# Two-layer diffusion backbone on one core: joins, squares and four adaLN slabs at the end of layer 0's experts

## The reference, cut to what matters

```python
for l in range(DEPTH):
    sh1, sc1, g1, sh2, sc2, g2 = split(silu(c) @ w_ada[l] + b_ada[l], 6)     # and the same of c_ctx
    h_lat = rms_norm(x, norm1_g[l]) * (1 + sc1) + sh1                        # h_ctx from ctx likewise
    h_ctx = rms_norm(ctx, norm1_g[l]) * (1 + csc1) + csh1
    y_lat, y_ctx = parallel_mixer(h_lat, h_ctx, w_in[l], ...)                # starts with h @ w_in[l]
    x = x + g1 * y_lat
    h2 = rms_norm(x, norm2_g[l]) * (1 + sc2) + sh2
    x = x + g2 * grouped_moe(h2, ...)      # 16 experts, the best 2 of a token's group; layer 0: ctx too
return rms_norm(x, final_g)
```

## Time and profile before

| | us |
|---|---|
| median of 3 runs (lowest, highest) | 1657.58 (1657.3, 1658.45) |
| the profiled execution | 1655.31 |
| its span, first to last instruction | 1653.4 |
| PE busy | 1495.7 (90%) |
| DVE / ACT / POOL busy | 817.5 / 616.7 / 233.7 |
| mean clock granted to PE | 0.959 of full |

### The profile page before, as it was taken

One profiled execution on the slowest core, in us unless ns is written; L12 is line 12 of the kernel. 1 busy time (PEld: TensorE's weight loads), 2 busy tenths in 40 slices (PEclk: granted clock), 3 DMA queues, 4 the chain that ended last, 5 costly groups with the idle time before them and its releaser, 6 DMA issues.

```text
span 1653.4 us, 16629 instructions
## 1 busy us (share of the span) xinstructions
PE 1495.7 (90%) x6502; PEld 959.8 (58%) x6502; DVE 817.5 (49%) x1111; ACT 616.7 (37%) x823; POOL 233.7 (14%) x204
## 2 busy tenths in 40 slices
PE   4999999998999967999999669999989987998884
PEld 1444665455888836888878434476548864433331
DVE  3145980676734457888887344482573123111103
ACT  3223441266333256778777242341151022111102
POOL 0004970400000002112110100281500000000000
PEclk8999999999999978999999879999999998999997
DMA  9511015395121546999999841114361456999991
GB/s 358 191 52 51 1 52 153 120 386 208 51 102 51 204 153 232 392 400 398 400 401 399 293 180 58 47 56 124 81 254 52 153 203 222 394 395 393 395 392 72
DMA packets 167142, 352.09 MB, mean 213 GB/s; under 512 B 21776, under 2 KB 22928, under 8 KB 167056
## 3 DMA queue, kind: packets, MB, share of 16 engines
q1 hardware_dynamic: 145472, 331.52, 54.1%
q0 software_dynamic: 3456, 12.58, 2.1%
q10 hardware_dynamic: 18128, 6.82, 2.0%
HBM read 339.38 MB, written 11.53 MB: 212 GB/s over the span
## 4 chain that ended last, share of the span: by engine, by line
PE 84%; DVE 6%; issue 3%; DMA 3%; ACT 2%; POOL 1%; SPq 0%; DVEq 0%; ACTq 0%; POOLq 0%
PE bank L543 15%; PE bank L554 7%; PE bank L1139 6%; PE bank L596 5%; PE bank L1161 4%; PE bank L916 3%; PE bank L922 3%; PE bank L913 3%; PE bank L620 3%; PE bank L514 2%; PE bank L733 2%; PE bank L736 2%; PE bank L729 2%; PE bank L1172 2%; PE bank L835 2%
## 5 line engine op out<-in xcount | busy, mean ns | idle before, releaser
L543 PE MATMUL bank<-hT,ring 128*128 128x512 f32 (+1 forms) x768 | 256.4, 492 | 10.2 <-ACT hT L1474 7.0
L2536 DVE TENSOR_TENSOR slab_lo<-slab,high 128x4096 fp32r<-128x4096 f32 x48 | 211.8, 4418 | 7.0 <-ACT high L1748 6.5
L543 PEld LDWEIGHTS bank<-hT,ring 128*128 128x128 f32 x768 | 146.8, 192 | 116.4 <-issue 98.9
L1748 ACT ACTIVATE high<-slab 128x4096 fp32r<-128x4096 f32 x48 | 174.3, 3635 | 26.0 <-PE bank L922 13.1
L1139 PE MATMUL bank<-narrow_slab,picked 128*64 128x512 f32 x256 | 114.4, 600 | 11.8 <-issue 11.6
L1140 PE MATMUL bank<-narrow_slab,picked 128*64 128x512 f32 x256 | 114.6, 601 | 0.0
L2011 POOL DMA_INDIRECT feed_rows<-token_table,slot_token x16 | 42.6, 2665 | 502.5 <-DVE slot_token L2476 307.8
L554 PE MATMUL bank<-ring,hT 128*128 128x512 f32 x256 | 110.5, 592 | 0.0
L596 PE MATMUL bank<-hT,ring 128*128 128x512 f32 (+1 forms) x256 | 104.7, 548 | 0.0
L554 PEld LDWEIGHTS bank<-ring,hT 128*128 128x128 f32 x256 | 48.6, 190 | 60.4 <-issue 60.3
L1139 PEld LDWEIGHTS bank<-narrow_slab,picked 128*64 128x64 f32 x256 | 34.7, 138 | 82.7 <-issue 82.2
(11 more groups left out here) (302 smaller groups left out, 2609.1 us busy)
## 6 DMA issues: line engine op xcount, KB each, us to landing
ring<-in_w_ada SPq DMA_DIRECT2D x24, 2048.0 KB, 13.0
ring<-in_w_in SPq DMA_DIRECT2D x24, 2048.0 KB, 9.0
slab<-in_w_gate SPq DMA_DIRECT2D x16, 2048.0 KB, 15.9
slab<-in_w_up SPq DMA_DIRECT2D x16, 2048.0 KB, 15.0
slab<-in_w_down SPq DMA_DIRECT2D x16, 2048.0 KB, 14.7
narrow_slab<-in_w_gate SPq DMA_DIRECT2D x16, 2048.0 KB, 18.0
narrow_slab<-in_w_up SPq DMA_DIRECT2D x16, 2048.0 KB, 22.0
narrow_slab<-in_w_down SPq DMA_DIRECT2D x16, 2048.0 KB, 19.3
```

What stands on the lines that cost most here:

```text
L543: mm = T.matmul(o[:, lo:TOK], w[:, k, c * P:(c + 1) * P], hT[:, k, lo:TOK], start=(k == 0), stop=(k == KT - 1))
L1748: S.activation(high[kind][:], w[:], ACT.Copy)\
L2536: V.tensor_tensor(low[:], w[:], high[kind][:].bitcast(f32), ALU.subtract)\
```

## The change

- The four adaLN slabs 16 to 19 leave the list `loads`. The slots that came free for them at the end of the experts now take `("in", 1, 3)` to `("in", 1, 6)`. The adaLN slabs get buffers of their own, `ada_slab`, over tiles that are dead by then; SP issues them after the gathers have landed, the fourth after the last join too, since it lies over `tok_rows[1]`. They signal in pairs: `ada_there0` for 16 and 17, `ada_there1` for 18 and 19.
- On PE the rows of 16 and 17 come after the transposes of `join_tokens` and ahead of `mean_square`; the rows of 18 and 19 and the turns of 16 and 17 after `mean_square` and ahead of the first projection; the turns of 18 and 19 after its first column block. ACT copies 16 and 17 after the root and 18 and 19 after `hT`; DVE adds all four to `mod` after the norm.
- DVE does all four joins ahead of both additions.
- The squares of this one norm are made by segments (16 pieces of 128x256, as soon as each piece of `xT` is there), and GpSimd sums them (14 additions) in place of DVE (7).
- Three semaphores of the kernel's start become one, `filled`, counted to three.

The diff, cut to its core:

```diff
@@ -229,6 +229,9 @@
...
     high = [fixed(f"high{i}", [P, SLOT], f32r, offset=(A0 + 44 * KB, A0 + 60 * KB, hT_at)[i]) for i in range(3)]
+    ada_slab = [fixed(f"ada_slab{i}", [P, SLOT], offset=A0 + (44, 60, 0, 76)[i] * KB) for i in range(4)]
+    square_late = fixed("square_late", [P, 2, TOK], offset=A0 + 32 * KB)
+    sum_late = fixed("sum_late", [P, TOK], offset=A0 + 36 * KB)
     hrow = fixed("hrow", [P, 4, D], offset=A0)
...
@@ -280,6 +283,15 @@
...
+        late_ada = range(16, 20)
...
+        def squares_before(count):
...
+            return KT * count + (KT if count > 2 else 0)
...
+        def sums_before(count):
+            return (KT - 1) * count + (KT - 1 if count > 2 else 0)
...
         def slot_of(key):
...
@@ -287,9 +299,6 @@
...
         for l in range(DEPTH):
-            if l == 1:
-                loads += ada_loads[16:20]
-                lane += range(SLOTS)
             loads += [("in", l, s) for s in (3, 4, 5, 6, 0, 1, 2, 7)]
...
@@ -506,21 +515,26 @@
...
                 key = ada_loads[n]
-                pe.wait_ge(*full(key))
-                w = slot(key).rearrange("p (k n) -> p k n", k=KT)
+                if n in late_ada:
+                    pe.wait_ge(sem[f"ada_there{(n - 16) // 2}"], 32)
+                    w = ada_slab[n - 16][:].rearrange("p (k n) -> p k n", k=KT)
+                else:
+                    pe.wait_ge(*full(key))
+                    w = slot(key).rearrange("p (k n) -> p k n", k=KT)
                 o = open_bank(key, "ada_row")
...
                 mm.then_inc(sem["psum_ready"], 1)
-                slot_spent[slot_of(key)] = (sem["psum_ready"], jobs[0])
+                if n not in late_ada:
+                    slot_spent[slot_of(key)] = (sem["psum_ready"], jobs[0])
...
                 if n == 0:
-                    pe.wait_ge(sem["pick2_ready"], 1)
+                    pe.wait_ge(sem["filled"], 3)
                 for j in range(4):
...
@@ -529,8 +543,8 @@
...
                 o = open_bank(key, "norm_std")
-                pe.wait_ge(sem["square_added"], (KT - 1) * (count + 1))
-                T.matmul(o[:, lo:TOK], ones, square_sum[:, lo:TOK], start=True, stop=True).then_inc(sem["psum_ready"], 1)
+                pe.wait_ge(sem["square_added"], sums_before(count + 1))
+                T.matmul(o[:, lo:TOK], ones, (sum_late if count == 2 else square_sum)[:, lo:TOK], start=True, stop=True).then_inc(sem["psum_ready"], 1)
...
@@ -569,10 +583,18 @@
...
                     ada_turn(3)
+                else:
+                    ada_rows(18)
+                    ada_turn(16)
+                    ada_rows(19)
+                    ada_turn(17)
                 for s, who in ((3, "q_ready"), (4, "k_sig"), (5, "k_sig")):
...
                         project(l, s, c, who, lo if s == 3 else 0)
+                        if l and s == 3 and c == 0:
+                            ada_turn(18)
+                            ada_turn(19)
                 pe.wait_ge(*full(("in", l, 6)))
...
@@ -1248,14 +1270,6 @@
...
                 if l == 0:
...
-                    pe.wait_ge(sem["y_kept"], 2 * N_EXPERTS)
-                    pe.wait_ge(*total(1, None, "x_added", phases[1][1] - 1, 4))
-                    for n in range(16, 20):
-                        ada_rows(n)
-                        if n > 16:
-                            ada_turn(n - 1)
-                    ada_turn(19)
                     join_tokens()
...
@@ -1263,7 +1277,12 @@
...
                         continue
-                    reader["experts", l, b] = ("tok_added", 16)
+                    reader["experts", l, b] = ("tok_added", 8 if b < 4 else 16)
+                if l == 0:
...
+                    turns[0] = 0
+                    ada_rows(16)
+                    ada_rows(17)
             if stop > 30:
...
@@ -1299,6 +1318,11 @@
...
                         sp.wait_ge(sem[f"tok_there{t}"], 32)
+                    for i in range(4):
+                        if i == 3:
+                            sp.wait_ge(sem["tok_joined"], 4)
+                        sp.dma_start(ada_slab[i][:].rearrange("p (k n) -> p k n", k=KT), source(ada_loads[16 + i])[0])\
+                            .then_inc(sem[f"ada_there{i // 2}"], 16)
                 while n < base:
...
@@ -1352,7 +1376,9 @@
...
-                    first_after = {i: slot_of(ada_loads[16 + i]) for i in range(SLOTS)}
+                    first_after = {i: min(m for m in range(slot_of(("in", 1, 3)), len(loads)) if lane[m] == i)
+                                   for i in range(SLOTS)}
+                    assert sorted(first_after.values()) == [slot_of(("in", 1, 3)) + i for i in range(SLOTS)]
                     for e in range(-1, N_EXPERTS):
...
@@ -1460,6 +1486,9 @@
...
                         .then_inc(sem["square_ready"], 1)
+                finish_norm(key, count, lo)
...
+            def finish_norm(key, count, lo):
                 act.wait_ge(*is_ready(key))
...
@@ -1491,12 +1520,28 @@
...
                 segs = segs_of[l]
-                norm(("ms", l, 0), 2 * l, 0, lambda k: (sem["tok_added"], KT + k + 1))
...
                 if l == 0:
+                    norm(("ms", 0, 0), 0, 0, None)
                     for n in range(4):
                         ada_keep(n)
+                else:
...
+                    act.wait_ge(sem["filled"], 2)
+                    S.activation(unused_std[:], epsv[:], ACT.Sqrt)
+                    for sg in range(2):
+                        for k in range(KT):
+                            act.wait_ge(sem["tok_added"], KT * sg + k + 1)
+                            if k >= 2:
+                                act.wait_ge(sem["square_added"], sums_before(2) + (KT - 1) * sg + max(1, k - 2))
+                            a = slice(sg * SEG, (sg + 1) * SEG)
+                            S.activation(square_late[:, k % 2, a], xT[:, k, a], ACT.Square).then_inc(sem["square_ready"], 1)
+                    finish_norm(("ms", 1, 0), 2, 0)
+                    ada_keep(16)
+                    ada_keep(17)
                 modulate(2 * l, 0, gain1[:, l], mod[:, l, 0:KT, :])
+                if l:
+                    ada_keep(18)
+                    ada_keep(19)
                 for c in range(4):
...
@@ -1938,8 +1983,6 @@
...
                 if l == 0:
-                    for n in range(16, 20):
-                        ada_keep(n)
                     join_tokens()
...
@@ -2024,6 +2067,15 @@
...
+                for sg in range(2):
+                    a = slice(sg * SEG, (sg + 1) * SEG)
+                    for k in range(1, KT):
+                        pool.wait_ge(sem["square_ready"], squares_before(2) + KT * sg + k + 1)
+                        if k > 1:
+                            pool.wait_ge(sem["square_added"], sums_before(2) + (KT - 1) * sg + k - 1)
+                        G.tensor_tensor(sum_late[:, a], square_late[:, 0, a] if k == 1 else sum_late[:, a],
+                                        square_late[:, k % 2, a], ALU.add).then_inc(sem["square_added"], 1)
...
@@ -2056,7 +2108,7 @@
...
             by_row = ident.rearrange("p (j c) -> p c j", c=32)
-            V.tensor_reduce(pick2[:], by_row[:, 0:2, :], AX.X, ALU.add).then_inc(sem["pick2_ready"], 1)
+            V.tensor_reduce(pick2[:], by_row[:, 0:2, :], AX.X, ALU.add).then_inc(sem["filled"], 1)
...
@@ -2119,8 +2171,6 @@
...
                 if l == 1:
-                    for k in range(KT):
-                        add_square(2, k, 0)
                     invert(2, 0)
...
@@ -2129,6 +2179,9 @@
...
                 link(V.memset(pb[:, :, 0:1], 0.0))
+                if l:
+                    for n in late_ada:
+                        ada_mod(n)
                 for way, (k_to, p_to) in enumerate(((kf, pf), (kb, pb))):
...
@@ -2580,11 +2633,9 @@
...
-                    join(0)
-                    join(1)
-                    join(2)
+                    for t in range(4):
+                        join(t)
                     add(0)
-                    join(3)
                     add(1)
...
@@ -2761,8 +2812,6 @@
...
                 if l == 0:
-                    for n in range(16, 20):
-                        ada_mod(n)
                     join_tokens()
```

More of the change, by code:

```diff
@@ L254, in build @@
     expert_table = nc.dram_tensor("expert_table", (N_EXPERTS * P, D), f32, kind="Internal").ap()
-    names = """const_loaded vec_loaded x_loaded tables_loaded bias_loaded out_stored psum_ready side_ready cond_zeroed cond_ready
-        pick2_ready ada_row ada_mod
-        epsv_ready lower_ready square_ready square_added norm_std normed_ready h_ready q_ready
+    names = """const_loaded vec_loaded x_loaded tables_loaded bias_loaded out_stored psum_ready side_ready filled cond_ready
+        ada_row ada_mod
+        lower_ready square_ready square_added norm_std normed_ready h_ready q_ready
         sig_ready k_sig log_in log_out v_ready naqk_ready rope_done sums_ready decay_in decay_out fac_ready
@@ L269, in build @@
```

(16 more changed lines are left out.)

## The result

| | before | with the change |
|---|---|---|
| median (lowest, highest), 9 runs each | 1657.48 (1653.22, 1658.49) | 1662.93 (1657.2, 1669.03) |
| the profiled execution, its span | 1655.31, 1653.4 | 1666.41, 1664.6 |
| mean clock granted to PE, profiled execution | 0.959 | 0.953 |

The ratio is 1.0038 with a 95% interval of 1.0021 to 1.0055: slower, by 5.5 us in the medians and 6.3 us by the ratio (interval 3.5 to 9.1), where 4.2 was forecast. Beside the last experiments the same kernel gave 1.0020 (1.0005 to 1.0034; median 1662.49 of 12 runs against 1658.98 of 30). The two intervals overlap between 1.0021 and 1.0034, or 3.5 to 5.6 us, and the forecast lies in that.

What follows compares the result with a forecast made beforehand. TensorE bounds the kernel (84% of the span); locally, PE waiting for late adaLN slabs moves the second block of layer 1's first projection from 975.1 to 979.3. That +4.2 on the 1657.6 median gives 1661.8 us, range 1659.4 to 1663.8.

Steps and rivals of the forecast that it cites:

- the fourth landing: Last of the four late adaLN transfers, expected at 966.3 us; rows 18 and 19 wait for it ahead of the projection.
- the half clock: After PE's idling before rows 18, PE was expected at half clock for 4.1 us from their start.
- xT complete, against before: End of the last additions into xT, expected at 950.9 instead of 953.6 us through joins first: 2.7 us earlier.
- rows 16 and 17: PE's adaLN rows ahead of the mean-square matmul, starting at the second landing near 955.5 and taking 6.1 us.
- mean-square matmul ends, against before: Matmul of the norm's summed squares, held behind PE's queue, expected to end at 962.7 instead of 961.8: 0.9 us later.
- rows 18, turn 16, rows 19, turn 17: PE's adaLN work ahead of layer 1's first projection, starting at 966.4 and expected to end at 973.9 us.
- marker: Start of the second column block (c = 1) of layer 1's first projection, expected at 979.3 instead of 975.1: +4.2 us.
- GpSimd's sums: The norm's 14 additions of squares, taken at 0.75 us each, expected to end at 956.0 us, 3.6 earlier than before.
- the second (slabs in time, pauses hide the rows): Slabs arrive in time at layer 1's start and the sums set the end: -1.8 us, 1655.8; chance 0.04.
- The first rival: PE's clock stays up through the pause at 963 to 966, or something later recovers part: +2.2 to +3.2; chance 0.14.
- The third (all four transfers land together): The four adaLN transfers share engines and end together at 966.3, delaying rows 16 and 17: +13.5 us, 1671; chance 0.03.
- The fourth rival (sums as the bound): GpSimd's additions, at 1.59 us each, end at 967.8 and set the projection's start: +9.9 us, 1667.5; chance 0.04.

Runs made afterwards that it cites:

- e1: The changed kernel with the four adaLN slabs loaded, read and turned where they were before the change; ratio 0.9992 against before, median 1657.19 us.
- e2: The kernel before with only the late adaLN slabs and their moved PE rows; joins, squares and sums as before; 1.0027 against before, median 1662.25 us.
- e4: The changed kernel with rows 16 to 19 reading w_in slabs already in the ring, without the adaLN transfers; 2682.74 us, unusable because routing changed.
- e7: The changed kernel's order on PE, ACT and DVE, but the four adaLN slabs stay in the ring as before; 0.9998 against before, median 1658.22 us.
- e3: The changed kernel with the rows of slabs 16 and 17 moved behind the mean-square matmul on PE; 1.0009 against before, median 1660.69 us.
- e5: The kernel before with one edit, all four joins ahead of both additions; 0.9978 against before, median 1656.09 us.
- e6: e1 with the squares in eight buffers and the sums shared by GpSimd and DVE; 0.9969 against before, median 1655.22 us.

## Why the prediction was right

The forecast was +4.2 us, 1661.8, by PE's rows waiting for the slabs' landings, with the second landing ahead of the mean square and the fourth ahead of the projection. e1, e2, e4 and e7 show this cause from both sides: take the slab part out, or its waits alone, and the loss is gone; keep it alone, and the loss is there in full. What e3 adds is that the loss has two parts, the wait for the fourth landing and the half clock behind the pause; the forecast had both. How near the number came is partly luck, since the two comparisons of the change with before, 5.5 and 3.5 us in the medians, themselves lie 2 us apart. Step by step, counted from the expert's end, so that an earlier shift doesn't enter:

| step | forecast | profile after |
|---|---|---|
| xT complete, against before | -2.7 | -2.9 |
| last sum, against before | -3.6 | -1.2 |
| landings 2 and 4, after the first issue | 13.6, 24.4 | 13.7, 25.4 |
| rows 16 and 17 | 6.1 | 6.4 |
| mean-square matmul ends, against before | +0.9 | +1.4 |
| rows 18, turn 16, rows 19, turn 17 | 7.5 | 9.0 |
| block 0, then turns 18 and 19 | 3.5, 1.9 | 3.6, 1.7 |
| marker | +4.2 | +6.6 (again: +5.0) |

Three terms were mis-sized. *The fourth landing* came 25.4 us after the first issue and not 24.4, in both profiles of the change; this is 1.0 of the 2.4 us by which the marker in the first profile lies behind the forecast, and its cause is open (e3 has 24.4). *GpSimd's sums* I took at 0.75 each; they came every 0.87 from start to start, each with a busy time of 0.72, and DVE's additions had no part in it, since the second seven, with DVE idle, took as long as the first. So the rule on the shared port in the Trainium skill, "SBUF — State Buffer", didn't come into play: the additions read one of their inputs from PSUM. (The prediction's working by that rule has a slip: 0.75 and 0.40 make 1.15 a sum and not 1.0, so 961.6 for the last sum, just ahead of the 961.7 at which rows 16 and 17 were to end.) Behind the first sum of each half there is another wait of 0.6 for ACT's square. It cost nothing here because the sums weren't what PE waited for, and 1.6 us in e1 against e5. *The half clock* behind the pause I ended 4.1 us after the start of rows 18; it ended 7.6 after it in one profile and 3.7 in the other. I had it at half from their start. In the first profile PE began rows 18 at full clock, fell to half 0.8 us later and stayed there until 976.6, though it was busy all the time; in the second the fall came 0.3 us after the start. My value lay near the second profile, my upper bound, +5.4, was 1.2 short of the first.

Of the rivals, the second (slabs in time, pauses hide the rows) said what e4 and e7 then measured: with the data there, the pieces fit, and the sums and hT set the end. Its price of -1.8 us was too good, +0.3 and +1.0 in the profiles, since it counted on the sums at 956.0. The first rival's bound, 10.9 us from the fourth landing to the marker at full clock, is e3's 11.0. The third (all four transfers land together) didn't occur: the landings came in order, 5.4 to 6.3 us apart. The Trainium skill, "DMA: Bandwidth & Descriptors", in "Queues, rings and completion order", leaves the order of completion open; the landings of this case came in order. The fourth rival (sums as the bound) didn't occur either.

The profiled executions differ by 11.2 us, of which the stage explains 6.6. Another 1.5 lie ahead of it, and 3.1 behind it. The first part is no sign of the change: the end of the expert's work lies between 919.9 and 923.4 us in the ten profiles, 922.4 and 923.4 in the change's two, but 920.3 in e2, which has the same slab part. Most of the last part can be placed. First and last start of the two groups around layer 1's second norm and router, before:

```profile
L835 PE MATMUL bank<-merged,ring x128: 379/379/483, 1327.1 to 1354.6; 128*128 128x256 f32 x128
...
L1139 PE MATMUL bank<-narrow_slab,picked x256: 592/592/1061, 1383.6 to 1620.1; 128*64 128x512 f32 x128
```

and after:

```profile
L857 PE MATMUL bank<-merged,ring x128: 379/379/483, 1336.2 to 1363.7; 128*128 128x256 f32 x128
...
L1161 PE MATMUL bank<-narrow_slab,picked x256: 592/592/1061, 1395.0 to 1631.1; 128*64 128x512 f32 x128
```

Until the first group the shift is 1336.2 - 1327.1 = 9.1, at the second 11.4: 2.3 us arise in a passage where PE has short pieces with pauses between, busy for 16.2 us of 28.6 before and for 18.4 of 30.9 after. Both kernels run the same instructions there, at a mean granted clock of 0.76 and 0.72. In the second profile of the changed kernel the way from the first group to the second is as long as in before (1333.0 to 1389.5, 56.5 us), so these 2.3 us belong to that one execution and not to the change. I tried nothing there; that the clock sets the difference is not shown. Such differences are why the stage was the better measure.

## What to carry to other kernels

Before work is moved out of what looks like a block on the critical chain, ask what would end last without it: here a row of gathers ran underneath, and moving 13.7 us of PE work away completed xT only 0.9 us earlier (e1 against e7), and the marker not at all. Work that fills a pause must have its data when the pause begins. If it waits for a transfer and stands in an in-order queue, everything behind it waits too, and the pause ahead of it can leave it at half clock, which cost another 1.6 to 3.9 us here. A serial sum is paid by the step, and the step on GpSimd was longer than its busy time (0.87 against 0.72 us), even with its input there: moving the whole sum there cost 1.6 us (e1 against e5), giving it half, with eight buffers for the squares, took 1.9 us off the stage (e6 against e5).

## What the runs showed of the hardware that was not expected

- The same seven pieces of work from rows 18 to the marker took 14.2, 12.6 and 14.9 us behind a pause of PE of 4.24, 4.53 and 5.75 us (the change, its second profile, e2), and 11.0 us without one (e3). The half clock came at no fixed place: 0.8 and 0.3 us *after* the work had begun again in the change's two profiles, and 2.1 us before it, in the pause, in e2. It lasted 6.8, 3.4 and 10.2 us, with PE busy in all of it but those 2.1 us.
- A GpSimd addition of 128x256 in a row where each waits for the one before came every 0.87 us, at 0.72 of busy time, whether ACT's squares were made in step with it (the change) or ahead of it (e6); a subtraction of that size in the scan, the free row of before, has 0.61.
- Single executions of one kernel on one core differed by up to 15 us here (1657.11 to 1672.38 in 12 runs of the changed kernel), and by 10.6 for before (1655.53 to 1666.13 in 30).
